# Forming h2 on VectorE from PSUM, clearing and biasing banks ahead of the first gather, in a one-layer diffusion step

## What is computed

```python
h = rmsnorm(x, g_ffn) * (1.0 + sc_f) + sh_f
logits = h @ w_router + b_router                      # 32 experts
top_vals, top_idx = lax.top_k(logits, 4)
combine = sum(one_hot(top_idx) * softmax(top_vals))
gu = h @ w_up[e] + b_up[e]                            # for each expert e
gate, up = min(gu[:, :1024], 7), clip(gu[:, 1024:], -7, 7)
y = ((up + 1) * gate * sigmoid(1.702 * gate)) @ w_down[e] + b_down[e]
x = x + gt_f * sum_e(combine[:, e] * y)
```

## Time and profile before

| | before |
|---|---|
| runs, us | 1158.14, 1161.99, 1162.92; median 1161.99 |
| the profiled execution, us | 1158.52 |
| its span, us | 1156.8 |
| mean granted TensorE clock | 0.981 |
| busy, share of the span | PE 91%, PEld 45%, DVE 29%, ACT 15%, POOL 5% |
| HBM | 459.15 MB in all, 397 GB/s on the mean |
| w_up chunks on the ring | 127 x 2048 KB, 26.9 us from issue to landing |
| w_down chunks on the ring | 63 x 2048 KB, 23.0 us |

### The profile page before, as it was taken

How to read it: one execution, slowest core, us unless ns; L and a number is a source line. 1 busy time by engine, 2 the same in 40 slices (tenths; PEclk the granted TensorE clock), 3 DMA queues, 4 the chain that set the end, 5 groups by cost and what they waited for, 6 DMA issues and landing times.

```text
span 1156.8 us, 13975 instructions
## 1 busy us (share of the span) xinstructions
PE 1056.0 (91%) x5704; PEld 520.2 (45%) x5704; DVE 334.7 (29%) x609; ACT 178.4 (15%) x323; POOL 61.9 (5%) x97
## 2 busy tenths in 40 slices
PE   6999999899999999999989898989898989898986
PEld 5987699834334343424343334343433343333322
DVE  5676877502313021202020202021212121212125
ACT  4453145501101010101010101010101010101011
POOL 5050000400000000000000000000000000000000
PEclk9999999899999999999999999999999999999999
DMA  9988977699999999999999999999999999999994
GB/s 309 377 240 329 388 286 316 276 367 425 420 403 429 426 429 427 429 428 429 427 429 429 429 428 428 430 427 429 428 429 427 429 429 429 428 427 423 422 420 195
DMA packets 58659, 459.15 MB, mean 397 GB/s; under 512 B 4805, under 2 KB 17161, under 8 KB 28057
## 3 DMA queue, kind: packets, MB, share of 16 engines
q1 hardware_dynamic: 57256, 455.12, 95.2%
q0 software_dynamic: 1168, 2.81, 1.0%
q10 hardware_dynamic: 192, 0.66, 0.2%
HBM read 456.99 MB, written 1.57 MB: 396 GB/s over the span
## 4 chain that ended last, share of the span: by engine, by line
PE 60%; DMA 33%; DVE 3%; SPq 2%; issue 1%; ACT 1%; POOL 0%; DVEq 0%; ACTq 0%
DMA ring<-in_w_down_dram 30%; PE ps L1842 17%; PE ps L1857 10%; PE ps L1779 6%; PE ps L1732 5%; PE ps L1743 5%; PE ps L1442 3%; DMA ring<-in_w_in_dram 2%; PE ps L1877 2%; PE ps L1772 1%; PE ps L1759 1%; DMA ring<-in_w_ada_dram 1%; PE ps L1497 1%; PE ps L1663 1%; PE ps L1498 1%
## 5 line engine op out<-in xcount | busy, mean ns | idle before, releaser
L1842 PE MATMUL ps<-ring,arena 128*64 128x512 f32 x1664 | 364.6, 594 | 17.4 <-DMA ring<-in_w_up_dram 17.3
L1857 PE MATMUL ps<-ring,arena 128*64 128x512 f32 x896 | 212.5, 630 | 50.1 <-DMA ring<-in_w_down_dram 50.1
L1842 PEld LDWEIGHTS ps<-ring,arena 128*64 128x64 f32 x1664 | 121.0, 137 | 244.3 <-issue 242.0
L1857 PEld LDWEIGHTS ps<-ring,arena 128*64 128x64 f32 x896 | 73.7, 145 | 188.6 <-issue 169.5
L1300 DVE TENSOR_TENSOR arena<-ps,arena 128x512 f32<-128x512 f32 x64 | 44.3, 692 | 297.4 <-PE ps L1743 297.4
L1281 DVE TENSOR_SCALAR arena<-ps 128x512 f32<-128x512 f32 x32 | 20.6, 686 | 258.9 <-PE ps L1842 220.2
L1779 PE MATMUL ps<-ring,arena 128*64 128x512 f32 x368 | 81.2, 594 | 1.0 <-DVE arena L1283 0.7
L1732 PE MATMUL ps<-arena 128*128 128x128 f32 x512 | 64.9, 286 | 1.7 <-DVE arena L1242 1.7
L1732 PEld LDWEIGHTS ps<-arena 128*128 128x128 f32 x512 | 62.9, 200 | 4.2 <-issue 4.2
L869 ACT ACTIVATE arena<-arena 128x512 f32<-128x512 f32 x32 | 19.6, 629 | 271.7 <-DVE arena L1281 271.7
L1269 DVE TENSOR_SCALAR arena<-arena,cur 128x64 f32<-128x64 f32 x64 | 11.9, 250 | 162.5 <-PE ps L1751 160.2
(11 more groups left out here) (277 smaller groups left out, 965.4 us busy)
## 6 DMA issues: line engine op xcount, KB each, us to landing
ring<-in_w_up_dram SPq DMA_DIRECT2D x127, 2048.0 KB, 26.9
ring<-in_w_down_dram SPq DMA_DIRECT2D x63, 2048.0 KB, 23.0
ring<-in_w_ada_dram SPq DMA_DIRECT2D x16, 1024.0 KB, 10.4
ring<-in_w_ada_dram SPq DMA_DIRECT2D x16, 512.0 KB, 9.8
ring<-in_w_in_dram SPq DMA_DIRECT2D x16, 512.0 KB, 9.6
ring<-in_w_in_dram SPq DMA_DIRECT2D x8, 1024.0 KB, 7.4
ring<-in_w_out_dram SPq DMA_DIRECT2D x4, 1024.0 KB, 6.6
ring<-in_w_pb_dram SPq DMA_DIRECT2D x2, 1024.0 KB, 8.4
```

The costliest lines, as they stand in the source:

```text
L1842: ins = mm(ps[CAP * a:CAP * a + CAP, n, :], xgT[:, h, kk, CAP * a:CAP * a + CAP], w[a][:, n * HALF:(n + 1) * HALF], start=False, stop=(kk ...
L1857: ins = mm(ps[CAP * a:CAP * a + CAP, YB + n, :], hT[:, f, CAP * a:CAP * a + CAP], w[a][:, n * HALF:(n + 1) * HALF], start=(f == 0), stop=( ...
```

## The change

- VectorE makes each of the four groups of h2 in one instruction, from PSUM times rstd plus the shift (`h2_out`); ScalarE's scalings and GpSimd's sums go, and with them `h2a`. Two groups stand between the mask and the ranks' result, two behind the one-hots.
- The banks: x2 * Af is turned into banks 2, 3, 5 and 7, x2 into 0, 1, 0, 1. The router's two sums share bank 6 (a matmul of the identity with zeros opens it), and so do the ranks; the two sums of squares lie in banks 0 and 1, and the first of them stands ahead of the last router block.
- TensorE turns two groups of x2 before the ranks and two behind them; `keep_busy(3, 4)` stands behind each.
- `up_bias(0)` stands ahead of the first gather, behind a wait for all four copies of x (three before).
- ScalarE's exponentials stand between its second and third copy of x. GpSimd clears the accumulator after `cur_ready`. The totals of the experts wait for h2.

```diff
@@ -360,6 +358,7 @@
         NT = [(n, t) for n in range(2) for t in range(2)]
+        AF_BANK, X2_BANK = (2, 3, 5, 7), (0, 1, 0, 1)
 
@@ -613,11 +612,6 @@
             nc.gpsimd.tensor_tensor(rstd, misc[:, 0:2], mhalf[:, :].to_broadcast([P, 2]), ALU.pow).then_inc(root_ready, 1)
-            for k_, (n, t) in enumerate(NT):
-                c = slice(n * HALF, (n + 1) * HALF)
-                pool.wait_ge(bc_read, 2)
-                pool.wait_ge(h2a_ready, k_ + 1)
-                nc.gpsimd.tensor_tensor(h2[:, t, c], h2a[:, t, c], h2[:, t, c], ALU.add).then_inc(h2_ready, 1)
 
@@ -636,6 +630,7 @@
             pool.wait_ge(x2_t, 4)
+            pool.wait_ge(cur_ready, 1)
             nc.gpsimd.memset(acc, 0.0).then_inc(acc_zero, 1)
@@ -824,16 +819,13 @@
             for k, (n, t) in enumerate(NT):
-                act.wait_ge(af_t, k + 1)
-                act.wait_ge(root_ready, 3)
-                nc.scalar.activation(h2a[:, t, n * HALF:(n + 1) * HALF], ps[:, 2 + 2 * t + n, :], ACT.Copy,
-                                     scale=rstd[:, t:t + 1]).then_inc(h2a_ready, 1)
-            act.wait_ge(top_ready, 1)
-            for t in range(2):
-                nc.scalar.activation(rt[:, t, 1, :], rt[:, t, 0, :], ACT.Exp, bias=misc[:, 4 + t:5 + t]).then_inc(e_ready, 1)
-            for k, (n, t) in enumerate(NT):
+                if k == 2:
+                    act.wait_ge(top_ready, 1)
+                    for g in range(2):
+                        nc.scalar.activation(rt[:, g, 1, :], rt[:, g, 0, :], ACT.Exp,
+                                             bias=misc[:, 4 + g:5 + g]).then_inc(e_ready, 1)
                 act.wait_ge(x2_t, k + 1)
-                nc.scalar.activation(x[:, t, n * HALF:(n + 1) * HALF], ps[:, 2 + 2 * t + n, :],
+                nc.scalar.activation(x[:, t, n * HALF:(n + 1) * HALF], ps[:, X2_BANK[k], :],
                                      ACT.Copy).then_inc(x_back, 1)
@@ -1210,12 +1202,12 @@
             dve.wait_ge(logit_done, 2)
-            V.tensor_scalar(misc[:, 0:2], ps[:, 0, 0:4:2], 1.0 / D, EPS, ALU.mult, ALU.add).then_inc(mean_ready, 1)
+            V.tensor_scalar(misc[:, 0:2], ps[:, 0:2, 0], 1.0 / D, EPS, ALU.mult, ALU.add).then_inc(mean_ready, 1)
             R = [rt[:, :, n, :] for n in range(8)]
...
             for t in range(2):
-                ins = V.scalar_tensor_tensor(out=rt[:, t, 0, :], in0=ps[:, 6 + t, 0:E], scalar=rstd[:, t:t + 1],
+                ins = V.scalar_tensor_tensor(out=rt[:, t, 0, :], in0=ps[:, 6, E * t:E * t + E], scalar=rstd[:, t:t + 1],
                                              in1=cst[:, t, :], op0=ALU.mult, op1=ALU.add)
@@ -1234,14 +1226,26 @@
 
+            def h2_out(k):
+                n, t = NT[k]
+                c = slice(n * HALF, (n + 1) * HALF)
+                dve.wait_ge(af_t, k + 1)
+                V.scalar_tensor_tensor(out=h2[:, t, c], in0=ps[:, AF_BANK[k], :], scalar=rstd[:, t:t + 1],
+                                       in1=h2[:, t, c], op0=ALU.mult, op1=ALU.add).then_inc(h2_ready, 1)
+
+            h2_out(0)
+            h2_out(1)
+
             pairs = tab[:, 0:PAIRS, :].rearrange("p q (w t b) -> p w t q b", w=2, t=2)
...
             dve.wait_ge(rank_done, 1)
-            link(V.scalar_tensor_tensor(out=R[7], in0=ps[:, 6:8, 0:E], scalar=1.0, in1=R[5], op0=ALU.add, op1=ALU.mult))
+            link(V.scalar_tensor_tensor(out=R[7], in0=ps[:, 6, 0:2 * E].rearrange("p (t n) -> p t n", t=2), scalar=1.0, in1=R[5], op0=ALU.add, op1=ALU.mult))
             link(V.tensor_scalar(pairs[:, 0], R[7].rearrange("p t (q b) -> p t q b", b=2), 1.0, None, ALU.subtract))
...
                             tab[:, 0, 0:4].unsqueeze(2).to_broadcast([P, 4, CAP]), ALU.is_equal).then_inc(oh_ready, 1)
+            h2_out(2)
+            h2_out(3)
             dve.wait_ge(e_ready, 2)
@@ -1667,10 +1671,12 @@
                     pe.wait_ge(cols_read, 4)
+                    pe.wait_ge(zeroed, 1)
+                    mm(ps[:, 6, 0:2 * E], ident[:, :], woT[:, 0, 0:2 * E], start=True, stop=False)
                 pe.wait_ge(x2T_ready, j + 1)
                 for t in range(2):
-                    ins = mm(ps[:, 6 + t, 0:E], x2T[:, j, t * P:(t + 1) * P], wrtA[:, t, j, :],
-                             start=(j == 0), stop=(j == KB - 1))
+                    ins = mm(ps[:, 6, E * t:E * t + E], x2T[:, j, t * P:(t + 1) * P], wrtA[:, t, j, :],
+                             start=False, stop=(j + t == KB))
                 if j == KB - 1:
@@ -1688,35 +1694,42 @@
                     router(j - 1)
+            pe.wait_ge(sqs_ready, KB - 2)
+            mm(ps[:, 0, 0:2], sqs[:, 0:P], ones[:, 0:2], start=True, stop=False)
             router(KB - 1)
-            pe.wait_ge(sqs_ready, KB - 2)
+            mm(ps[:, 1, 0:2], sqs[:, P:TOK], ones[:, 0:2], start=True, stop=False)
             pe.wait_ge(sq_ready, KB)
             for t in range(2):
-                mm(ps[:, 0, 2 * t:2 * t + 2], sqs[:, t * P:(t + 1) * P], ones[:, 0:2], start=True, stop=False)
-                ins = mm(ps[:, 0, 2 * t:2 * t + 2], sq[:, 3, t * P:(t + 1) * P], ones[:, 0:2], start=False, stop=True)
+                ins = mm(ps[:, t, 0:2], sq[:, 3, t * P:(t + 1) * P], ones[:, 0:2], start=False, stop=True)
             ins.then_inc(logit_done, 1)
 
-            def to_rows(src, n, t):
+            def to_rows(src, k, bank):
+                n, t = NT[k]
                 for j in range(4 * n, 4 * n + 4):
-                    ins = tp(ps[:, 2 + 2 * t + n, (j % 4) * P:(j % 4 + 1) * P], src[:, j, t * P:(t + 1) * P], ident[:, :])
+                    ins = tp(ps[:, bank, (j % 4) * P:(j % 4 + 1) * P], src[:, j, t * P:(t + 1) * P], ident[:, :])
                 return ins
...
             pe.wait_ge(x2af_ready, KB)
-            for n, t in NT:
-                to_rows(x_chan, n, t).then_inc(af_t, 1)
-            for k, (n, t) in enumerate(NT):
-                pe.wait_ge(h2a_ready, k + 1)
-                to_rows(x2T, n, t).then_inc(x2_t, 1)
+            for k in range(4):
+                to_rows(x_chan, k, AF_BANK[k]).then_inc(af_t, 1)
+            pe.wait_ge(mean_ready, 3)
+            for k in range(2):
+                to_rows(x2T, k, X2_BANK[k]).then_inc(x2_t, 1)
+            keep_busy(3, 4)
 
...
             mm(ps[:, 6, 0:E], tri[:, :], rt[:, 0, 5, :], start=True, stop=True)
-            mm(ps[:, 7, 0:E], ones[:, :], rt[:, 0, 5, :], start=True, stop=False)
-            mm(ps[:, 7, 0:E], tri[:, :], rt[:, 1, 5, :], start=False, stop=True).then_inc(rank_done, 1)
+            mm(ps[:, 6, E:2 * E], ones[:, :], rt[:, 0, 5, :], start=True, stop=False)
+            mm(ps[:, 6, E:2 * E], tri[:, :], rt[:, 1, 5, :], start=False, stop=True).then_inc(rank_done, 1)
+            for k in range(2, 4):
+                pe.wait_ge(x_back, k - 1)
+                to_rows(x2T, k, X2_BANK[k]).then_inc(x2_t, 1)
+            keep_busy(3, 4)
 
...
 
-                pe.wait_ge(x_back, 4)
+                pe.wait_ge(h2_ready, 4)
                 mm(ps[:, 5, 0:E], ones[:, :], rt[:, 0, 5, :], start=True, stop=False)
@@ -1782,7 +1795,8 @@
 
-                up_bias(R)
+                if second_half is None:
+                    up_bias(R)
                 for kk in range(KB):
@@ -1929,7 +1943,8 @@
             pe.wait_ge(h2_ready, 2)
-            pe.wait_ge(x_back, 3)
+            pe.wait_ge(x_back, 4)
+            up_bias(0)
             gather(0, 0, FIRST[0])
```

More of the change, by code:

```diff
@@ L213, in layer_kernel @@
         x_chan = x[:, :, :].rearrange("p a (b c) -> p (a b) c", c=TOK)
-        h2a = region(4096, 2, D)
         sq = region(8960, 4, TOK)
@@ L315, in layer_kernel @@
         x2T_ready, sq_ready, sqs_ready = sem("x2T_ready"), sem("sq_ready"), sem("sqs_ready")
-        x2af_ready, af_t, h2a_ready, x2_t, x_back = (sem("x2af_ready"), sem("af_t"), sem("h2a_ready"), sem("x2_t"),
-                                                     sem("x_back"))
+        x2af_ready, af_t, x2_t, x_back = sem("x2af_ready"), sem("af_t"), sem("x2_t"), sem("x_back")
         br_done, merged_ready = sem("br_done"), sem("merged_ready")
```

## The result

The changed kernel takes 1152.51 us (median of 7 runs, 1151.86 to 1154.46); the kernel before, in 7 runs beside it, 1158.14 (1157.37 to 1162.92). The ratio is 0.9949, with a 95% interval from 0.9937 to 0.9961: about 5.9 us less; the interval lies on both sides of a gain of 0.5%. The profiled execution took 1154.46 us, span 1152.7, against 1158.52 and 1156.8 before. I had forecast 1159.6 with a range from 1154.7: the direction was right, the gain was more than twice mine, and the time fell out of the range.

A forecast was written before the change was run, and what follows sets the result against it. TensorE's first up block was taken to bound the kernel through weight-slot releases: at 229.8 instead of 232.24, 2.4 us earlier, off the shown median of 1162.0 gives 1159.6 us; range 1154.7 to 1162.5.

The forecast's parts named there:

- The bound, and the way from the first block to the end: TensorE's first up block sets the weight-slot releases; each microsecond earlier reaches the end, up to 4.95 us.
- the first hole: Weight stream at 234 to 238 us, short of 429 GB/s: 3.28 us lost; forecast to be nearly shut.
- the second: Hole in the weight stream at 330 to 334 us: 1.67 us lost; forecast to remain, shorter.
- The hold of VectorE by GpSimd: GpSimd's four sums hold VectorE's comparisons and scans before the mask; without them minus 2.1 and 1.7 us.
- Sixteen transposes as before: 217.22 to 220.36: Start of TensorE's list ahead of the ranks: transposes take 3.14 us, as in the profile before.
- the clock does not fall at 218: Rival: TensorE's clock stays up through the transposes; gain 3.8 us, time 1158.2, chance 0.15.
- My cap of 4.95 us: Limit on the gain at the end: the two holes in the weight stream, 3.28 and 1.67 us.
- the clock late or low again: Rival: TensorE's clock comes back late or falls again in the gather; gain 0.9 or 0.8, time 1161.2, chance 0.14.
- the slower one: Rival: fillers on a TensorE clock that stays low up to the first block; loss 2.8 us, 1164.8, chance 0.05.
- the hold that stays: Rival: VectorE's steps are slow of themselves, mask at 224.8 as before; gain 0.4 us, 1161.6, chance 0.08.
- the bare copy: ScalarE's copy of the gathered rows, before the first block, no longer under the biases: plus 0.64 us.
- the swap of biases and gather: TensorE's biases ahead of the first gather: by itself gives back 0.7 us of the gain.

The follow-up runs named there:

- pool_sums: The changed kernel with h2 made as before by ScalarE's scaling and GpSimd's sums; 1159.0 us, ratio 1.0004 to the kernel before.
- no_fillers: The changed kernel without its six filler matmuls, both groups taken out; 1153.8 us, ratio 0.9954 to the kernel before.
- early_no_fill: The changed kernel with the first gather ahead of the wait for the copies of x and the biases, and no fillers; 1152.5 us, ratio 0.9956 to the kernel before.
- before_again: The kernel before, unchanged, run again for a second trace; one run, 1159.1 us.

## Why the prediction was wrong

*The bound, and the way from the first block to the end*: right. Both releases moved by the same 3.5 us, the first hole nearly closed, the second stayed (no shorter, though I had said it would be), and 2.6 us of pure delay came out as 1.9 at the end of a trace and 3.1 in the medians.

*The hold of VectorE by GpSimd*: right in cause and size. Minus 2.1 and 1.7 us forecast behind the sums, measured 3.9; minus 0.2 ahead of them, measured 0.29; each of the four steps took 0.22 or 0.23. The rival in which the steps are slow of themselves has fallen.

*"Sixteen transposes as before: 217.22 to 220.36"*: here the sum failed. I took the low clock of one execution for a property of the kernel, and so put TensorE's list 1.9 us behind the mask. In all seventeen other traces of the study the sixteen transposes ran at full clock, 1.94 or 1.95 us by the timeline, where this one has 3.35. With that the list meets the mask within 0.24 us, and the first block starts 10.66 behind the transposes instead of my 12.6. Of these 1.9 us, 1.36 lie in the sixteen transposes (1.78 instead of 3.14) and 0.47 in the eight behind them (0.87 instead of 1.34), half of which I had at the low clock too. My own rival, "the clock does not fall at 218", had a gain of 3.8 us; measured are 3.9 to the release (18.28 less 14.35), and 4.2 with the 0.29 ahead of the start. It had a chance of 0.15; by the seventeen traces it should have been the forecast. What made the clock fall at 218 in that one execution stays open.

*The execution that the sum was made against*: its release at 18.28 is not the usual one. The two others have 19.5, since there the low clock falls on gather, biases and first block. That is 1.2 us at the release which no term of the sum had. I wrote of this fall only "My sum has the first fall as it was and no second one", and counted its absence on gather and biases, but not that it is commonly longer than in this profile. What it gave to the time is not known: at the ends of the spans, 939.4 against 939.5 and 939.6 us, it does not show.

*The time*: of the 7.1 us between 1159.6 and 1152.5, the gain is 5.6 - 2.4 = 3.2; the other 3.9 is the base. The median of three runs, 1162.0, was high; of seven it is 1158.1. The range had its lower end at the profiled execution less 3.8, so it missed by 2.2. My cap of 4.95 us, the two holes together, was kept by the traces (4.8) and not by the medians (5.6).

*The rivals*: the clock late or low again, at 0.14, the slower one at 0.05, and the hold that stays were all wrong for the change. They are right for its neighbours: pool_sums and no_fillers show the clock falling in this stretch.

*The rule on transposes*: by the Trainium skill, "TensorE: Matmul & The Clock Gate", section "PE-mode transpose", the full clock does not engage on them. In the first profile it rose from 0.50 to 1.00 at about 221.2 us while TensorE ran nothing else, and in the change it was 1.00 through 24 of them. That speaks against the rule as it stands. In no_fillers it fell at 224 after 6 us of transposes, short rank matmuls and 1.7 us of idle time, so the runs cannot exclude that transposes count for less than other work.

*What the edits were costed at*: the bare copy was counted right, 0.69 us of waiting; the swap of biases and gather costs 1.1 us by trace, where I had 0.7. Fillers 1.30 a group, as summed. The wait for all copies of x was covered, as said.

## What to carry to other kernels

Before a sum is made against a profile, ask of each stretch at low clock whether it would be there in another execution: a fall that nothing in the code explains is to be taken out of the sum, and one behind a long idle wait of TensorE, here 3.3 us for the mask, is to be priced on whatever comes next. GpSimd's adds, 4.95 us of them beside a chain of short VectorE steps, cost the chain 3.7 to 3.9 us; one VectorE instruction that reads PSUM and adds on the way out replaced two engines' work and freed the chain. Where a stream of weights sets the end, what counts is the time of the first slot release, and an idle wait of TensorE ahead of it may be worth filling: in the kernel before, with waits of 3.3 and 1.65 us, it gave 1.4 us; in the change, with waits under 1 us, it gave nothing to the median, and better than filling them was to put real work there, the gather.

## What the runs showed of the hardware

- The low clock landed in different places in executions of the same program: transposes and part of the gather once, gather, biases and first block twice. Its place made 1.2 us up to the first release (18.28 against 19.5), and without fillers 2.8 (15.37 against 18.21).
- In the eleven traces with at least one filler group (three matmuls of 128x256 in float32, 1.3 us) and no idle wait of TensorE over 1 us, the clock was 1.00 from the transposes to the first block. One trace without any filler, early_no_fill, had that too; two others had not. In pool_sums, with a filler group and then an idle wait of 3.39 us, it fell. Why, stays open.
- VectorE steps of 64 elements with both inputs in SBUF, 0.22 us alone, took up to 1.3 beside GpSimd's sums and ended 0.1 behind them; a step with one input in PSUM, started 0.9 us into GpSimd's clearing of the accumulator in before_again, took 0.22, and the step behind it, a `tensor_scalar` from SBUF to SBUF, 0.68 instead of 0.20. The Trainium skill has this in "SBUF — State Buffer", section "Who interferes with whom": a VectorE instruction with at most one SBUF input, outside the 2-port modes, does not contend with GpSimd. The step with an input in PSUM agrees, and so does the count of line 1228 in the first profile, 0.22 us at 222.12 within the sums. The step that took 0.68 has one SBUF input as well and was held; the section names `tensor_scalar` among those that can enter a 2-port mode, and no row here shows which mode it ran in.
- Two scans of 32 elements take 0.46 us together when nothing holds them.
